# Two transformer blocks on one core: no wait for the attention's stores, another order of vector work in the gated linear attention, and mixer tiles three steps ahead of their product

## The chip, the cores and the metric

One core of one Trainium2 chip runs the whole program in one launch. The metric is the device time of an execution in microseconds (us). The engines are TensorE (PE in the profile; PEld is its weight load), VectorE (DVE), ScalarE (ACT), GpSimd (POOL) and SyncE (SP), whose queue issues the DMA transfers. Each engine runs its own list of instructions in the order in which they were written, and waits on semaphores for the others.

## The reference, cut to what matters

The program computes two blocks, one after the other, on 1024 tokens of width 1024, in float32. The first is a gated delta-rule mixer (8 heads of 128) and a squared-ReLU MLP (width 4096). The second has a softmax attention (8 query heads of 64, 2 key heads, 1280 keys: 256 of a context and 1024 of the sequence), a bidirectional gated linear attention ("GLA", called hgrn2 in the reference, 4 heads of 128), an output projection of both, and a SwiGLU MLP (2 x 2816).

```
def gated_deltanet(...):                       # first block
    ...  8 heads, chunks of 128 tokens in the kernel, output o
    return (o * rsqrt(mean(o*o)+eps) * norm_w * silu(z)) @ w_out

def hgrn2_prep(q, i, f, lb_d):                 # second block, GLA
    fg = lb_d + (1.0 - lb_d) * sigmoid(f)
    qh = silu(q) * 128 ** -0.5
    return qh, 1.0 - fg, i, log(fg)            # queries, keys, values, log decay
S_t = diag(f_t) S_{t-1} + k_t v_t^T;  o_t = S_t^T q_t     # forward and backward
o = rmsnorm(o_f + flip(o_b), gain) * silu(g)
x = x + mx[2] * (concat([att_x, hg_x]) @ w_out)
```

Both parts are linear in the values i, so the factor 128 ** -0.5 may stand on the queries or on the values.

## The kernel before, in words

Activations are kept feature-major: a tile is 128 features by 1024 tokens. A large product runs in three passes (high and low halves of weights and of activations), in "units" of one 128-wide output tile: a unit has 8 k-steps, each in two "pieces". For every unit SP loads 512 KB of weights (`sp_weights`, L461), ACT copies the high half (`act_weights`, L478) and DVE subtracts to get the low half (`dve_weights`, L486). PE may start a unit when DVE's part is done. There are three buffers of each.

The order of the work is written out by hand. While a recurrent chain runs, with many short hand-overs between PE, ACT, DVE and POOL, large products of the next head fill PE. They come from a generator of steps (`DeltaSide` for the first block's mixer, `GlaSide` for the second's). Every engine calls the same generator at the same points (`side.fill(n)` runs n steps, `side.until(x)` runs them until x is ready). A step gives PE one piece; the other engines get their own share of the unit at its start and end. A `yield` without work before it is a step in which PE gets nothing. When the chain is over, `side.finish()` runs what is left.

The last steps of both generators are `mix_steps` (L151): the first two output tiles (i = 0, 1) of the output projection, over k-tiles 0 to 6 of the mixer's output. These k-tiles lie in device memory and are loaded again (`sp_mix`). `mix_tile(k)` makes ACT copy the high half of k-tile k (L1310) and DVE subtract the low half (L1316); `mix_piece` is PE's share (by `gemm_piece`, L497), four or two matmuls of 512 columns. `mix_tile(0)` waits for the end of the last unit before, since it overwrites that unit's activations. k-tile 7 comes from the last head at the end (L1323, L1328, and L1354 on PE). In the first block the steps begin in head 7, at the fourth turn of its two half chains (`delta_halves`, L813). There L1125 and L1127 are small DVE sums and L1139 is the first DVE copy of the triangular inversion; L930 on PE and L1180 on DVE end the head. In the second block they begin in GLA head 3, at the sixth of its seven levels.

The softmax attention (`*_attend`, L2092 to L2229) makes 160 steps of scores, exponentials and products with the values; SP stores its output tiles (L2099) to device memory. At its end each engine calls `after_attend` (L2103), which waits for all events of this stage and for all of these stores. Only then does an engine enter the GLA, whose tiles lie in the same on-chip memory. In the GLA the projections of head 0 come first (L2806 is PE's piece, L2849 is ACT's evacuation into the head's tile, by `gla_into`, L2334; L2816 and L2866 transpose the values).

A GLA head then runs so. DVE waits for the queries of the head, for the store of the previous head's output (`glast`) and for POOL, scales the queries (L2456), makes the decay factors and keys of both directions (L2459, L2461, twice) and adds the keys (L2463, event "kk"). PE multiplies keys and queries (L2279, event "dg"). DVE puts the diagonal (L2445) and makes the two decayed queries (L2469, event "q0"). Then come 7 levels: PE L2292, DVE and POOL multiply keys (L2423), queries (L2430) and factors (L2433), DVE puts the level's part (L2445), ACT makes the interleaved keys (L2404, L2407). Then follow transposes of the keys (L2304), the states (L2310 on PE, L2486 and L2492 on DVE), the output (L2319 to L2321) and its norm and gate (L2501 to L2514, event "of"). SP stores it (L2254). `gla_fill` is the number of fill steps at each point; in head 3 it is halved.

Of the kernel before, what the change touches and what calls it, by code (L numbers as in the profile page):

```python
# [10 lines left out]
ALU = mybir.AluOpType  # L11
# [7 lines left out]
KT = 8  # L19
# [131 lines left out]
def mix_steps(on):  # L151

    on.mix_tile(0)
    for k in range(KT - 1):
        if k + 1 < KT - 1:
            on.mix_tile(k + 1)
        for part in range(2):
            for i in range(2):
                on.mix_piece(i, k, part)
                yield None  # L160
# [165 lines left out]
class Kernel:  # L326
# [1765 lines left out]
    def sp_attend(self, e):  # L2092
        P, A, V, G = self.at
        for i in range(16):
# [3 lines left out]
            for p in range(2):  # L2098
                e.dma_start(self.scratch[0][64 * p:64 * p + 64, 2 * g:2 * g + 2, qc],  # L2099
                            ao[:, :, p, :]).then_inc(*self.attst[i % 4].up(i, p))  # L2100
        self.after_attend(e)

# [6 lines left out]
    def pe_attend(self, e):  # L2109
# [21 lines left out]
        for t in range(162):  # L2131
# [14 lines left out]
            if t >= 2:  # L2146
# [3 lines left out]
                if b == 0 and i >= 2:  # L2150
                    e.wait_ge(*V.at("of", i - 2))
                e.matmul(O[i % 2], self.vx[:, b, 64 * g:64 * g + 128], self.prob[(t - 2) % 4], start=b == 0,  # L2152
                         stop=b == 9).then_inc(*P.up("pv", t - 2))
        self.after_attend(e)

    def act_attend(self, e):
        P, A, V, G = self.at
        MX, MT, S, O = self.attend_banks()
        for t in range(160):
# [3 lines left out]
            e.activation(self.prob[t % 4], S[t % 3], ACT.Exp, scale=0.125).then_inc(*A.up("ex", t))  # L2163
        self.after_attend(e)

    def dve_attend(self, e):
# [28 lines left out]
        for i in range(17):  # L2195
# [18 lines left out]
            if i < 15:  # L2214
                maxima(i + 1, 2)
                maxima(i + 1, 3)
                shift(i + 1)
        self.after_attend(e)

    def pool_attend(self, e):  # L2220
# [4 lines left out]
        for i in range(16):  # L2225
            qc, g, r, base = self.attend_rows(i)
            e.wait_ge(*(P.at("s", 10 * (i - 2) + 9) if i >= 2 else G.at("zero", g)))
            e.tensor_copy(self.qx[g][r], self.qs[g][r, :, qc].bitcast(F32)).then_inc(*G.up("qx", i))
        self.after_attend(e)  # L2229

# [16 lines left out]
    def sp_gla(self, e):  # L2247
        V = self.gs[2]
        e.dma_start(self.masks, self.a["masks"]).then_inc(*self.maskl.up("gla"))
        j0 = UNIT["win", 10]  # L2250
# [15 lines left out]
    def pe_gla(self, e):  # L2266
# [4 lines left out]
        for h in range(4):  # L2271
# [4 lines left out]
            side.fill(self.gla_fill(h, 8))  # L2276
            e.wait_ge(*V.at("kk", h))
            for n in range(8):
                ins = e.matmul(blk(D0, n), blk(B["sq"], n), blk(B["hq"], n), start=True, stop=True)  # L2279
# [54 lines left out]
    def gla_into(self, e, u, c):  # L2334
        P, A, V, G = self.gs
        i = u[1] - 6
        part, h = i // 4, i % 4
        if part == 1:
            if h >= 2:
                e.wait_ge(*P.at("o", h - 2))  # L2340
            return self.iv[h % 2].rearrange("p a b -> p (a b)")[:, c], ACT.Copy
# [93 lines left out]
    def dve_gla(self, e):  # L2435
# [11 lines left out]
        for h in range(4):  # L2447
            side.stage = 4 * h
            side.until((h, "hq"))
            f = {n: B[f"f{n}{h % 2}"] for n in "fb"}  # L2450
            k, q = {"f": B["kf"], "b": B["kb"]}, {"f": B["qf"], "b": B["qb"]}
            e.wait_ge(*A.at("ev", ("win", 6 + h), 1))
            if h:
                e.wait_ge(*self.glast.at(h - 1))
                e.wait_ge(*G.at("up", h - 1, 6))
            e.tensor_scalar(B["hq"], B["hq"], 128.0 ** -0.5, None, ALU.mult)  # L2456
            for d, n in enumerate("fb"):
                j = 4 * d + h
                e.tensor_scalar(f[n], f[n], self.olb[:, j:j + 1], self.lb[:, j:j + 1], ALU.mult, ALU.add).then_inc(*V.up())  # L2459
                e.wait_ge(*V.last())  # L2460
                e.tensor_scalar(k[n], f[n], -1.0, 1.0, ALU.mult, ALU.add).then_inc(*V.up())  # L2461
            e.wait_ge(*V.last())
            e.tensor_tensor(B["sq"], k["f"][:, TC:TA], k["b"][:, TC:TA], ALU.add).then_inc(*V.up("kk", h))  # L2463
            side.fill(self.gla_fill(h, 8))
            e.wait_ge(*P.at("dg", h))
            side.fill(self.gla_fill(h, 3))
            put(self.con("ident"), D0, "put", h, "d")
            for n in "fb":
                ins = e.tensor_tensor(q[n], B["hq"], f[n][:, TC:TA], ALU.mult)  # L2469
# [356 lines left out]
class ActSide:  # L2826
# [27 lines left out]
    def turned(self, u):  # L2854
# [3 lines left out]
        for j in range(3):  # L2858
            n = min(4, 10 - 4 * j)
            if u == ("win", 5):  # L2860
# [5 lines left out]
            e.activation(out[:, 4 * j:4 * j + n, :], s.ps[:, 512 * j:512 * j + 128 * n].rearrange("p (b m) -> p b m", b=n),  # L2866
                         ACT.Copy).then_inc(*self.sig[1].up("tv", u, j))

# [175 lines left out]
```

## Time and profile before

| | us |
|---|---|
| median of 3 runs | 3335.62 (3332.84 to 3340.41) |
| the profiled execution's own time | 3333.01 |
| its span | 3331.2 |
| PE busy | 3100.7 (93%) |
| DVE busy | 1553.6 (47%) |
| ACT busy | 1002.6 (30%) |
| POOL busy | 433.9 (13%) |
| matmuls of the large products, L497 | 1474.4 in 5928 |
| matmuls of the projections, L2806 | 363.9 in 1584 |

The span is the time from the first to the last instruction; 1.8 us of the execution lie around it. Busy time of PE counts a matmul from start to a modelled end, so it says where PE had work, and not that it ran at its peak. The mean granted clock of PE was 0.973 of full speed.

### The profile page before, as it was taken

What the parts mean: (1) busy time and instruction counts of PE and PEld (TensorE: products, weight loads), DVE (VectorE), ACT (ScalarE), POOL (GpSimd) and SP (SyncE); (2) the same over time, 40 slices, a digit from 0 to 9 for tenths busy, and PEclk for the clock granted to TensorE, in tenths of its full rate; (3) what the DMA queues carried; (4) which work ended last, traced back from release to release, by engine and by line L of the source; (5) the groups of instructions that cost most, each with busy time, mean ns of one, the idle gap of its engine ahead of it and who ended that gap; (6) DMA issues with size and microseconds to landing.
All of it is one profiled execution on the core that took longest, in us unless ns stands there. A gap on an engine that the chain in (4) does not pass through costs nothing. (4 is left out here: it accounts for less than half of the span.)

```text
span 3331.2 us, 36380 instructions
## 1 busy us (share of the span) xinstructions
PE 3100.7 (93%) x15051; PEld 2518.8 (76%) x15051; DVE 1553.6 (47%) x1912; ACT 1002.6 (30%) x1440; POOL 433.9 (13%) x343
## 2 busy tenths in 40 slices
PE   7899999979999999999688998989879999999998
PEld 5788888867788888887565666877767788888886
DVE  7566656652664543333456761654463322222223
ACT  5555555542211111112423332222222211111111
POOL 4222223221000000001100000332131000000001
PEclk9999999999999999999888999999999999999999
DMA  3111111112233331112110001010012111111111
GB/s 124 33 45 45 45 45 45 45 64 102 89 108 120 114 97 49 50 46 87 42 51 5 9 10 41 20 38 32 26 58 100 42 47 50 46 51 45 51 43 59
DMA packets 77237, 184.78 MB, mean 55 GB/s; under 512 B 7056, under 2 KB 29072, under 8 KB 77072
## 3 DMA queue, kind: packets, MB, share of 16 engines
q1 hardware_dynamic: 77072, 182.44, 17.5%
q8 instruction: 120, 1.97, 0.3%
q14 instruction: 45, 0.37, 0.0%
HBM read 163.87 MB, written 15.79 MB: 54 GB/s over the span
## 5 line engine op out<-in xcount | busy, mean ns | idle before, releaser
L497 PE MATMUL ps<-b 128*128 128x512 f32 x5928 | 1474.4, 399 | 46.4 <-DVE b L1316 15.0
L497 PEld LDWEIGHTS ps<-b 128*128 128x128 f32 x5928 | 1091.3, 190 | 259.4 <-issue 26.8
L1512 PE MATMUL ps<-b 128*128 128x512 f32 x2592 | 608.5, 395 | 0.5 <-DVE b L1643 0.5
L1512 PEld LDWEIGHTS ps<-b 128*128 128x128 f32 x2592 | 485.1, 187 | 119.0 <-DVE b L1643 1.0
L486 DVE TENSOR_TENSOR b<-b 128x1024 fp32r<-128x1024 f32 (+1 forms) x206 | 254.7, 1237 | 326.9 <-ACT b L478 319.9
L2806 PE MATMUL ps<-b 128*128 128x512 f32 (+1 forms) x1584 | 363.9, 386 | 37.1 <-DVE b L1866 14.4
L478 ACT ACTIVATE b<-b 128x1024 fp32r<-128x1024 f32 (+1 forms) x206 | 215.1, 1045 | 562.7 <-PE ps L1512 463.8
L2806 PEld LDWEIGHTS ps<-b 128*128 128x128 f32 x1584 | 283.6, 197 | 94.8 <-issue 42.7
L1381 POOL TENSOR_TENSOR b<-b 128x1024 f32<-128x1024 f32 x24 | 57.5, 2397 | 1642.7 <-ACT b L1387 1642.3
L1558 ACT ACTIVATE b<-ps 128x1024 f32<-128x1024 f32 x54 | 55.4, 1025 | 389.2 <-PE ps L497 389.2
L2152 PE MATMUL ps<-b 128*128 128x512 f32 x320 | 163.0, 592 | 0.0
L1659 DVE TENSOR_TENSOR b<-b,ps 128x1024 f32<-128x1024 f32 x64 | 78.1, 1220 | 168.5 <-PE ps L1512 168.5
L2163 ACT ACTIVATE b<-ps 128x512 f32<-128x512 f32 x160 | 95.3, 597 | 149.2 <-PE ps L2145 149.2
L1564 ACT ACTIVATE b<-b 128x1024 fp32r<-128x1024 f32 x54 | 57.3, 1061 | 261.5 <-DVE b L1638 216.5
L1661 DVE SCALAR_TENSOR_TENSOR b<-ps,b 128x1024 f32<-128x1024 f32 x48 | 61.6, 1284 | 149.6 <-PE ps L1512 149.6
L1640 DVE TENSOR_TENSOR b<-b 128x1024 f32<-128x1024 f32 x32 | 39.2, 1225 | 183.1 <-ACT b L1558 183.1
L2176 DVE TENSOR_REDUCE b<-ps 128x1 f32<-128x1280 f32 x64 | 95.3, 1489 | 46.6 <-PE ps L2120 46.2
L1223 POOL TENSOR_TENSOR b<-b 128x256 f32<-128x256 f32 x96 | 82.6, 864 | 198.7 <-DVE b L1111 115.7
L2752 DVE SCALAR_TENSOR_TENSOR b<-b 128x1024 f32<-128x1024 f32 x72 | 105.3, 1463 | 0.8
L1638 DVE TENSOR_TENSOR b<-b,ps 128x1024 f32<-128x1024 f32 x22 | 26.9, 1221 | 166.2 <-PE ps L497 162.5
L2144 PE MATMUL ps<-b 128*128 128x512 f32 x160 | 98.2, 614 | 0.0
L1643 DVE TENSOR_TENSOR b<-b 128x1024 fp32r<-128x1024 f32 x54 | 66.2, 1225 | 60.8 <-ACT b L1564 60.8
(291 smaller groups left out, 3297.1 us busy)
## 6 DMA issues: line engine op xcount, KB each, us to landing
b<-in_down SPq DMA_DIRECT2D x52, 512.0 KB, 3.6
b<-in_mod SPq DMA_DIRECT2D x96, 256.0 KB, 2.7
b<-in_gu SPq DMA_DIRECT2D x44, 512.0 KB, 3.6
b<-scratch SPq DMA_DIRECT2D x38, 512.0 KB, 4.4
b<-in_dn_in SPq DMA_DIRECT2D x32, 512.0 KB, 4.9
b<-in_up SPq DMA_DIRECT2D x32, 512.0 KB, 3.7
b<-in_win SPq DMA_DIRECT2D x26, 512.0 KB, 4.0
scratch<-b SPq DMA_DIRECT2D x18, 512.0 KB, 3.0
```

The source lines that it names most:

```text
L478: e.activation(self.whi[j % SPL][:, 0:cols], self.raw[j % RAW][:, 0:cols], ACT.Copy).then_inc(*self.wh.up(j))
L486: e.tensor_tensor(self.wlo[j % SPL][:, 0:cols], self.raw[j % RAW][:, 0:cols], self.whi[j % SPL][:, 0:cols].bitcast(F32), ALU.subtract).the ...
L497: ins = e.matmul(ps[:, c], w, h[:, k, c], start=first and k == 0 and i == 0, stop=last and k == KT - 1 and i == 2)
L1223: e.tensor_tensor(out, own, m.broadcast_to([128, 4, 64 >> lv, 1 << lv]), ALU.mult).then_inc(*G.up("m", h, lv, f))
L1512: ins = e.matmul(ps[:, c], w, u[:, at[k], c], start=k == 0 and p == 0, stop=k == n - 1 and p == 2)
L1659: e.tensor_tensor(x, x, ps, ALU.add).then_inc(*V.up("down", f, i))
L2144: e.matmul(S[t % 3], blk(self.ks[g], b), self.qs[g][:, :, qc], start=True, stop=False)
L2152: e.matmul(O[i % 2], self.vx[:, b, 64 * g:64 * g + 128], self.prob[(t - 2) % 4], start=b == 0, stop=b == 9).then_inc(*P.up("pv", t - 2))
L2163: e.activation(self.prob[t % 4], S[t % 3], ACT.Exp, scale=0.125).then_inc(*A.up("ex", t))
L2176: e.tensor_reduce(mx[:, j:j + 1], MX, AX.X, ALU.max).then_inc(*V.up("mx", i, j))
L2752: e.scalar_tensor_tensor(out=dst, in0=k.d_pad[c % 2][:, t:t + T], scalar=cw[:, t:t + 1], in1=dst, op0=ALU.mult, op1=ALU.add).then_inc(*V.u ...
L2806: ins = e.matmul(self.bank[p], (hi, hi, lo)[i], x, start=k == 0 and i == 0, stop=last)
```

## The change

There are four edits.

1. `after_attend` is no longer called by PE, DVE and POOL at the end of the attention. ACT calls it before its first evacuation of head 0's values (the first write into a tile of the GLA), SP at the start of `sp_gla`. In its old place SP calls `sp_weights` with a bound that the projections before have reached already.
2. In `dve_gla` the factors, keys and their sum are made as soon as both gates of the head are projected (`side.until((h, "b"))`), with a wait for the evacuated gates, ahead of the waits for the queries, for the previous head's store and for POOL. These three waits now stand before the decayed queries (L2469). PE waits for the evacuated queries itself before L2279.
3. The queries are not scaled (L2456 goes). ACT scales the values by the same factor as it evacuates their transpose (L2866).
4. `mix_steps` starts with three steps in which PE gets nothing: `mix_tile(0)` in the first, `mix_tile(1)` in the second, none in the third. The later tiles keep their place relative to the pieces.

```
 def mix_steps(on):
     on.mix_tile(0)
+    yield None
+    on.mix_tile(1)
+    yield None
+    yield None
     for k in range(KT - 1):
-        if k + 1 < KT - 1:
+        if 0 < k < KT - 2:
             on.mix_tile(k + 1)
...
 def sp_attend(self, e):
-        self.after_attend(e)
+        self.sp_weights(e, UNIT["win", 10] + 4)
 # pe_attend, act_attend, dve_attend, pool_attend:
-        self.after_attend(e)
 def sp_gla(self, e):
         V = self.gs[2]
+        self.after_attend(e)
         e.dma_start(self.masks, self.a["masks"])...
 # pe_gla
             e.wait_ge(*V.at("kk", h))
+            e.wait_ge(*A.at("ev", ("win", 6 + h), 1))
 # gla_into
         if part == 1:
+            if h == 0 and c.start == TC:
+                self.after_attend(e)
 # dve_gla
         for h in range(4):
-            side.stage = 4 * h
-            side.until((h, "hq"))
             f = {n: B[f"f{n}{h % 2}"] for n in "fb"}
             k, q = {"f": B["kf"], "b": B["kb"]}, {"f": B["qf"], "b": B["qb"]}
-            e.wait_ge(*A.at("ev", ("win", 6 + h), 1))
-            if h:
-                e.wait_ge(*self.glast.at(h - 1))
-                e.wait_ge(*G.at("up", h - 1, 6))
-            e.tensor_scalar(B["hq"], B["hq"], 128.0 ** -0.5, None, ALU.mult)
+            side.stage = 4 * h
+            side.until((h, "b"))
             for d, n in enumerate("fb"):
                 j = 4 * d + h
+                e.wait_ge(*A.at("ev", ("win", 14 + j), 2))
                 e.tensor_scalar(f[n], f[n], self.olb[...], self.lb[...], ALU.mult, ALU.add)
                 e.wait_ge(*V.last())
                 e.tensor_scalar(k[n], f[n], -1.0, 1.0, ALU.mult, ALU.add)
             e.wait_ge(*V.last())
             e.tensor_tensor(B["sq"], k["f"][:, TC:TA], k["b"][:, TC:TA], ALU.add).then_inc(*V.up("kk", h))
+            side.until((h, "hq"))
             side.fill(self.gla_fill(h, 8))
             e.wait_ge(*P.at("dg", h))
             side.fill(self.gla_fill(h, 3))
             put(self.con("ident"), D0, "put", h, "d")
+            e.wait_ge(*A.at("ev", ("win", 6 + h), 1))
+            if h:
+                e.wait_ge(*self.glast.at(h - 1))
+                e.wait_ge(*G.at("up", h - 1, 6))
             for n in "fb":
                 ins = e.tensor_tensor(q[n], B["hq"], f[n][:, TC:TA], ALU.mult)
 # ActSide.turned
-                         ACT.Copy)
+                         ACT.Copy, scale=128.0 ** -0.5)
```

## Rows read from the trace of the kernel before

**Rows 1.** page, section 1: busy time of each engine, share of the span, instructions.
```profile
PE 3100.7 (93%) x15051; PEld 2518.8 (76%) x15051; DVE 1553.6 (47%) x1912; ACT 1002.6 (30%) x1440; POOL 433.9 (13%) x343
```

**Rows 2.** waits of TensorE's matmuls, 2010 to 2560: us in total, times, longest.
```profile
PE ps L2279 <- DVE b L2463: 17.8, 4, 7.3
...
PE ps L2806 <- DMA scratch<-b: 7.1, 1, 7.1
PE ps L497 <- DVE b L1316: 5.4, 1, 5.4
```

**Rows 3.** the same view, 676 to 752 (delta head 7 and what follows).
```profile
PE ps L497 <- DVE b L1316: 9.6, 1, 9.6
...
PE ps L1354 <- DVE b L1328: 1.4, 1, 1.4
PE ps L930 <- DVE b L1173: 0.9, 1, 0.9
```

**Rows 4.** timeline at the attention's end: start us, us, instruction, [idle before <-releaser].
```profile
2005.76 13.56 SPq L2099 DMA_DIRECT2D scratch<-b  x4
...
2011.20 2.74 PE L2152 MATMUL ps<-b 128*128 128x512 f32 x6
...
2021.02 16.93 PE L2806 MATMUL ps<-b 128*128 128x512 f32 x72 [7.08 <-DMA scratch<-b]
...
2024.79 1.23 DVE L486 TENSOR_TENSOR b<-b 128x1024 fp32r<-128x1024 f32 x1 [6.72 <-DMA b<-in_masks]
```

**Rows 5.** windows: stretch, length, busy us (count) by engine, TensorE clock, DMA.
```profile
693.00:747.80 54.80, 47.69 (x306) 39.15 (x304) 27.97 (x63) 22.01 (x54) 12.28 (x12) 1.00 0.07 20
...
2021.00:2027.00 6.00, 5.98 (x17) 4.93 (x18) 1.23 (x1) 1.06 (x1) 0.00 (x0) 0.50 0.50 165
```

**Rows 6.** timeline, GLA head 0: the keys' product.
```profile
2088.05 2.05 PE L2279 MATMUL ps<-b 128*128 128x128 f32 x16 [1.47 <-DVE b L2463]
```

**Rows 7.** timeline, change from GLA head 0 to head 1.
```profile
2184.84 1.28 DVE L2514 SCALAR_TENSOR_TENSOR b<-b 128x1024 f32<-128x1024 f32 x1
...
2189.20 0.69 DVE L2456 TENSOR_SCALAR b<-b 128x1024 f32<-128x1024 f32 x1 [3.08 <-DMA scratch<-b]
...
2194.64 3.47 PE L2279 MATMUL ps<-b 128*128 128x128 f32 x16 [5.64 <-DVE b L2463]
...
2196.81 1.23 DVE L486 TENSOR_TENSOR b<-b 128x1024 fp32r<-128x1024 f32 x1 [2.22 <-ACT b L478]
...
2198.15 1.32 DVE L2445 COPY_PREDICATED b<-b,ps 128x1024 f32<-128x1024 uint32 x1
...
2201.76 2.92 PE L2292 MATMUL ps<-b 128*128 128x128 f32 x16 [1.37 <-DVE b L2469]
```

**Rows 8.** timeline, change to head 2 (first row) and to head 3.
```profile
2304.92 2.05 PE L2279 MATMUL ps<-b 128*128 128x128 f32 x16 [3.36 <-DVE b L2463]
...
2401.73 1.28 DVE L2514 SCALAR_TENSOR_TENSOR b<-b 128x1024 f32<-128x1024 f32 x1
...
2411.52 3.78 PE L2279 MATMUL ps<-b 128*128 128x128 f32 x16 [7.32 <-DVE b L2463]
```

**Rows 9.** timeline, GLA head 3 where the output projection begins.
```profile
2451.87 2.35 DVE L1316 TENSOR_TENSOR b<-b 128x1024 fp32r<-128x1024 f32 x2
...
2458.01 0.69 DVE L2430 TENSOR_TENSOR b<-b 128x512 f32<-128x512 f32 x1 [3.05 <-PE ps L2292]
...
2490.72 4.82 PE L497 MATMUL ps<-b 128*128 128x512 f32 x20
```

**Rows 10.** timeline, delta head 7 where the output projection begins.
```profile
684.98 3.20 DVE L1316 TENSOR_TENSOR b<-b 128x1024 fp32r<-128x1024 f32 x2
...
687.19 2.04 PE L497 MATMUL ps<-b 128*128 128x512 f32 x4 [9.59 <-DVE b L1316]
...
694.20 0.23 DVE L1139 COPY b<-b 128x128 f32<-128x128 f32 x1 [2.56 <-PE ps L876]
```

**Rows 11.** line 1316: instructions, duration ns min/median/max, first and last start.
```profile
L1316 DVE TENSOR_TENSOR b<-b x14: 1172/1221/2062, 685.0 to 2488.8; 128x1024 fp32r<-128x1024 f32 x14
```

More of the change, by code:

```diff
@@ L153, in mix_steps @@
     on.mix_tile(0)
+    yield None
+    on.mix_tile(1)
+    yield None
+    yield None
     for k in range(KT - 1):
-        if k + 1 < KT - 1:
+        if 0 < k < KT - 2:
             on.mix_tile(k + 1)
@@ L2100, in sp_attend @@
                             ao[:, :, p, :]).then_inc(*self.attst[i % 4].up(i, p))
-        self.after_attend(e)
+        self.sp_weights(e, UNIT["win", 10] + 4)
     def after_attend(self, e):
@@ L2153, in pe_attend @@
                          stop=b == 9).then_inc(*P.up("pv", t - 2))
-        self.after_attend(e)
     def act_attend(self, e):
@@ L2163, in act_attend @@
             e.activation(self.prob[t % 4], S[t % 3], ACT.Exp, scale=0.125).then_inc(*A.up("ex", t))
-        self.after_attend(e)
     def dve_attend(self, e):
@@ L2217, in dve_attend @@
                 shift(i + 1)
-        self.after_attend(e)
     def pool_attend(self, e):
@@ L2228, in pool_attend @@
             e.tensor_copy(self.qx[g][r], self.qs[g][r, :, qc].bitcast(F32)).then_inc(*G.up("qx", i))
-        self.after_attend(e)
     GLA_ORDER = {"f": list(range(9)), "b": [1, 0, 9, 8, 7, 6, 5, 4, 3]}
@@ L2248, in sp_gla @@
         V = self.gs[2]
+        self.after_attend(e)
         e.dma_start(self.masks, self.a["masks"]).then_inc(*self.maskl.up("gla"))
@@ L2277, in pe_gla @@
             e.wait_ge(*V.at("kk", h))
+            e.wait_ge(*A.at("ev", ("win", 6 + h), 1))
             for n in range(8):
@@ L2338, in gla_into @@
         if part == 1:
+            if h == 0 and c.start == TC:
+                self.after_attend(e)
             if h >= 2:
@@ L2447, in dve_gla @@
         for h in range(4):
-            side.stage = 4 * h
-            side.until((h, "hq"))
             f = {n: B[f"f{n}{h % 2}"] for n in "fb"}
             k, q = {"f": B["kf"], "b": B["kb"]}, {"f": B["qf"], "b": B["qb"]}
[L2452 to L2456, printed above, removed]
+            side.stage = 4 * h
+            side.until((h, "b"))
             for d, n in enumerate("fb"):
                 j = 4 * d + h
+                e.wait_ge(*A.at("ev", ("win", 14 + j), 2))
                 e.tensor_scalar(f[n], f[n], self.olb[:, j:j + 1], self.lb[:, j:j + 1], ALU.mult, ALU.add).then_inc(*V.up())
@@ L2463, in dve_gla @@
             e.tensor_tensor(B["sq"], k["f"][:, TC:TA], k["b"][:, TC:TA], ALU.add).then_inc(*V.up("kk", h))
+            side.until((h, "hq"))
             side.fill(self.gla_fill(h, 8))
@@ L2467, in dve_gla @@
             put(self.con("ident"), D0, "put", h, "d")
+            e.wait_ge(*A.at("ev", ("win", 6 + h), 1))
+            if h:
+                e.wait_ge(*self.glast.at(h - 1))
+                e.wait_ge(*G.at("up", h - 1, 6))
             for n in "fb":
@@ L2866, in turned @@
             e.activation(out[:, 4 * j:4 * j + n, :], s.ps[:, 512 * j:512 * j + 128 * n].rearrange("p (b m) -> p b m", b=n),
-                         ACT.Copy).then_inc(*self.sig[1].up("tv", u, j))
+                         ACT.Copy, scale=128.0 ** -0.5).then_inc(*self.sig[1].up("tv", u, j))
 class DveSide:
```

## The prediction

> **What bounds the kernel now.** I read the page first: PE is busy in 93% of the span [rows 1]. So a change off PE counts only where PE waits, or where PE runs at half clock behind a wait. Next I read PE's own waits in the two stretches that the diff touches. In the GLA the longest are those for the keys' sum (17.8 us, 4 times), for the attention's stores (7.1, once) and for the first tile of the output projection (5.4, once) [rows 2]. In delta head 7 it is that first tile again (9.6, once), and behind it two small ones of 1.4 and 0.9 [rows 3]. Each is then looked up in the timeline, for what stood ahead of the late instruction on its own engine. All in all the diff touches 17.8 + 7.1 + 5.4 + 9.6 = 39.9 us of stalls. The sum is made against the profiled execution: 3331.2 us of span and 1.8 around it, 3333.0. The median of three runs, 3335.6, lies 2.6 above that.
>
> **Edit 1, the attention's end.** PE's last product ends at 2013.9 and the first projection begins at 2021.0, when the last stores have landed [rows 4]. The weights of the first two units are made already, and PSUM is free. After the change PE goes on at once: 7.1 us less. The projection then began at the 1.2 GHz level: 6.0 us with a granted clock of 0.50 [rows 5], work that takes 3.0 us at 2.4 GHz. With no pause there is no reason for that fall: 3.0 less. Sum: 10.1.
> What is late next? ACT takes over the wait, ahead of its first evacuation. Behind it are queued that evacuation and later weight copies; PE waits for the evacuation. The projection takes 16.93 - 3.0 = 13.9 us, so it ends at 2027.9, some 7 us after the stores. The wait is hidden; if the stores landed 10 us later it would cost 3. SP issues the load of the masks after the same stores as before, and DVE makes the third unit's low half behind it, 2024.8 to 2026.0 [rows 4]. PE needs it after two units, at 2013.9 + 2 x 13.9 = 2041.7, so this is hidden as well. The moved SP call issues nothing. Bounds: 7.1 (the clock falls anyway) to 10.1; I take 10.1.
>
> **Edits 2 and 3, the heads' beginnings.** Head 0: PE waits 1.47 us for the keys' sum [rows 6]. Its gates are evacuated one projection earlier, so DVE's work lies beside the queries' projection: 1.5 less.
> Head 1: DVE ends the head before at 2186.1, waits 3.08 us for its store, scales queries for 0.69, and makes factors and keys until 2194.6 [rows 7]. The first two go from this place, 3.8, and 4.75 are left of the 8.5. PE had sat idle for 5.64, so this is all gain at the keys' product. Is it kept until the levels? The diagonal on DVE waits for that product and, through a fill step, for one weight split (L486), which starts when ACT is through its key copies and a weight copy, also released by the keys' sum. It ended 3.4 us after the sum [rows 7], and will again. The diagonal and the queries follow. So the first level, at 2201.76, comes 3.8 earlier. The store has landed by 2189.2, before the decayed queries need their tile (about 2195.7): the moved wait is hidden, by 6 us.
> Head 2: the same step, but PE waited only 3.36 [rows 8]; no weight split stands in between here, and I take 3.4.
> Head 3: DVE ended at 2403.0, so the sum comes at about 2407.8 in place of 2411.5. The keys' product ran 3.78 us at half clock [rows 8] and held the diagonal until 2415.3; now the weight split holds it, until 2407.8 + 3.4 = 2411.2. That gives 4.1.
> The factor on the values rides on a copy that is made in any case. The trace shows no such copy with a factor; its bound is from 0 to the 0.69 of the scaling that goes [rows 7], three per head, beside other waits; I take 0. PE's added wait for the evacuated queries comes 8 or 4 fill steps after the projection: 0, at most about 1 in head 0. Sum: 1.5 + 3.8 + 3.4 + 4.1 = 12.8. Bounds: 6 (half of it is met by the next link of the chain, since the wait for the decayed queries, 1.37 in head 1, stays) to 15.
>
> **Edit 4 in GLA head 3.** PE sat 5.4 us before the first piece; level 7 had to wait behind it [rows 2]. Now level 7 is issued first. DVE becomes the limit: after level 6 it splits weights and tile 0, then multiplies the keys and waits for PE. Gone from its chain are half of the two tile splits (2.35 / 2) and the 3.05 of idle before the level's queries [rows 9]: 4.2. But three steps of PE's work, which lay here, move to the end. By the order of the pieces the steps now left over are of 4, 2 and 2 matmuls, at 4.82 / 20 = 0.24 each [rows 9]: 1.9. The 20 matmuls at the end covered the last tile's preparation fully (there is no wait for it there), so nothing absorbs them. Net 2.3. Bounds: -2 (the chain meets other waits and the three steps are pure cost) to 4.2.
>
> **Edit 4 in delta head 7.** PE's first piece started at 687.19 after 9.59 us. It needed DVE's first tile split, which ended about 687, and DVE's arrival there was not set by PE [rows 10]. So this piece starts no earlier. What changes is the work around it: the second half chain's transposes, and both halves' next ones, pass ahead of it and fill the pause. The chain's next link on DVE (L1139) stood at 694.20. Now it follows the first piece (2.04 at half clock) and one short transpose group (about 0.4): 687.2 + 2.0 + 0.5 = 689.7. DVE's own list reaches it in time: split until 687.0, two small sums of 0.9, the second split 1.2, 689.1. So the chain is 4.5 ahead. From 693 to 747.8 PE is busy for 47.7 of 54.8 us [rows 5] with the same steps at the same points, so the lead is passed on. At the end come three steps more, 8 matmuls, 1.9 us; the 0.9 before L930 [rows 3] absorbs half. Net 4.5 - 1.0 = 3.5. The 1.4 before the last tile stays, being DVE's. Bounds: -1 (no lead, the work only displaced, 1.0 exposed) to 6.5 (clock stays up).
> A rule on the split's length: line 1316 takes 1.22 at the median, and 2.06 at its longest, here in head 7 [rows 11]. The Trainium skill, GPSIMD Engine Reference, section 1 "Specifications", has GpSimd share its SBUF interfaces with VectorE, with contention for DVE instructions with two SBUF inputs. By that rule the first split stays long, since the change moves nothing of GpSimd's work away; if it dropped to 1.22 the sum would be 0.8 larger. I leave it long.
>
> **Sum.** 10.1 + 12.8 + 2.3 + 3.5 = 28.7. The profiled execution would take 3333.0 - 28.7 = 3304.3, a median like the one shown 3306.9. I say 3305.5, between them.
>
> **Rivals.**
> A. *The pieces are missed.* Removing three steps of fill under two latency-bound chains gives nothing or costs: -1 and -2 in place of 3.5 and 2.3, so 28.7 - 8.8 = 19.9, at 3314. For it: PE has only about 7 us of idle in 693 to 747.8, so the displaced steps find little room. Against it: both waits are ended by work queued on DVE, that is there in the rows.
> B. *The heads' waits move on.* The keys' sum comes early but the decayed queries are then late, behind the weight split, the store or ACT: half of the 12.8 is lost, 3312. For it: the wait before the first level was there each time. Against: all that stands ahead of it is released by the same sum.
> C. *The handover is hidden anyway*, or the edit does not do what it says: ACT, now holding the wait, stops PE at its first evacuation, or PE waits for the third unit. Then the 10.1 goes, 3315.6. Against it are the 7 and 15 us of slack.
> D. *The clock gives more.* After the pauses in heads 1 and 3 and in head 7 PE ran at the lower level; if it no longer falls there, 3 in the delta head and 3 to 5 in the GLA come on top: 3298.
> E. *Slower.* In head 7 the long stall made PE fall to half clock and it came back by 693. In the new order it falls in the shorter pause, has no large piece in turn 4, and stays at the 1.2 GHz level through the whole chain. Four matmuls of a piece took 2.04 at that level [rows 10] against 4 x 0.24 + 0.2 = 1.2 at the other, a factor of 1.7; on 47.7 us of work that is 33, at 3305.5 + 33 = 3338, slower. It decides from 41 us at half clock on (28.7 / 0.7). Against it: the same work in 693 to 747.8 was granted 1.00 throughout [rows 5].
>
> **How the numbers follow.** Forecast 0.60, its own range 3299 to 3311; A 0.11; B 0.10; C 0.05; D 0.10; E 0.02; nothing to be measured 0.02. Two measurements of this kernel are told apart from about 0.2%, 6.7 us. The range goes from D's far side to C and A together with a part of B: 3293 to 3321. What is left out is mostly E, pairs of A, B and C, and terms that I have not seen. Faster by over 0.2%: 0.94; within it: 0.03; slower: 0.03.
>
> **What would show it.** PE goes from the attention's last product to the first projection within 1 us, and all of that projection runs at clock 1.00; its transposes wait no longer than now. PE's waits for the keys' sum fall from 17.8 to about 5 (heads 1 and 3: about 2 and 3.6; heads 0 and 2: none). The first levels of heads 1 to 3 come 3 to 4 us closer to the end of the head before. In GLA head 3 PE's level 7 comes before any L497; the pause of 5.4 is replaced by two of 1.5 and 3.5. In delta head 7 the pause before the first piece is 4 to 5, and the pieces after the last head's output are 16 matmuls in place of 8. It would be wrong if a wait of over 3 us appeared before a first level or before L2816, or if the stretch between the fourth turn of head 7 and the last tile were not shorter.

## The result, and the profile after

The changed kernel took 3310.3 us (median of 4 runs, 3306.1 to 3311.3) against 3335.8 for the kernel before on the same chip (4 runs, 3332.8 to 3340.4): a ratio of 0.992, 95% interval 0.990 to 0.994. The forecast was 3305.5, with its own range of 3299 to 3311 and 3293 to 3321 in all, so the result lies at the upper edge of the first. Taken again beside other kernels, the same code took 3308.6 against 3337.0, ratio 0.9913 (0.9899 to 0.9927). All executions behind the medians here are fast ones, and the single slow one, 8833.1 us with the kernel that has the wait for the stores put back, is left out. The profiled execution took 3311.3, with a span of 3309.3: 21.9 less than before. The changed lines stand a few lines lower: L497 is now L501, L1316 is L1320, L2279 is L2281, L2292 is L2294, L2469 is L2474, L2806 is L2811, L2152 is L2156, L486 is L490, L1139 is L1143, L1354 is L1358, L2304 is L2306, L2430 is L2434, L2445 is L2449, L2492 is L2497, L2514 is L2519; L2463 stays.

The page's first section, kernel after, beside [rows 1]:

```profile
PE 3106.2 (94%) x15051; PEld 2523.6 (76%) x15051; DVE 1549.6 (47%) x1908; ACT 1003.0 (30%) x1440; POOL 435.5 (13%) x343
```

As many products as before and four DVE operations less, the four scalings of the queries. PE's busy time is 5.5 us higher: those are the same products, a few more of them at half clock (121.9 us of PE's busy time lie in stretches of half clock, in place of 109.7). So not all of PE's idle time that went came off the span.

I cut both executions at instructions that both have. D runs in delta head 7 from PE's last value transposes to the first product of the last k-tile (L1354 before). H runs from the start of the attention's last products to the keys' product of GLA head 0. K1, K2, K3 run from the broadcast of the norms (L79) to the first level's product of GLA heads 1, 2, 3. G runs in GLA head 3 from the sixth level's product to the first product of the last k-tile.

| stretch | before | after | gain | forecast |
|---|---|---|---|---|
| D | 72.30 | 66.25 | 6.05 | 3.5 |
| H | 76.85 | 65.23 | 11.62 | 10.1 + 1.5 |
| K1, K2, K3 | 19.30, 18.13, 20.21 | 15.42, 14.53, 16.00 | 3.9, 3.6, 4.2 | 3.8, 3.4, 4.1 |
| G | 50.06 | 51.68 | -1.6 | +2.3 |
| all the rest | 3074.4 | 3080.2 | -5.8 | 0 |

The touched stretches give 27.7, against 28.7 forecast. The rest is the same instructions in the same order, and is longer by 2.3 ahead of D, by 2.2 between D and H and by 1.4 elsewhere. It differs by such amounts between executions of one code: the stretch between D and H took 1265.6 in this one and 1264.1 in the second profile of the same kernel, 1261.8 and 1265.4 in the two profiles of another, and from 1258.0 to 1265.6 over all the profiles here. There is only one profile of the kernel before, so that the change adds nothing there is likely and not shown.

Waits of PE's matmuls, kernel after, 1980 to 2560 (us in total, times, longest), beside [rows 2]:

```profile
PE ps L2294 <- DVE b L2474: 8.9, 4, 2.7
...
PE ps L2281 <- DVE b L2463: 4.0, 2, 3.6
...
PE ps L2306 <- DVE b L2434: 3.2, 1, 3.2
...
PE ps L2294 <- DVE b L2434: 2.5, 2, 1.5
...
PE ps L501 <- DVE b L1320: 0.4, 1, 0.4
PE ps L2306 <- DVE b L2449: 0.4, 1, 0.4
```

The 17.8 for the keys' sum are 4.0, the 7.1 for the stores are no longer there, and the 5.4 before the first piece have become 1.5 before level 7 (L2294, of the 2.5), and 3.2 and 0.4 behind it, before the transposes of the keys (L2306). The forecast had two pauses of 1.5 and 3.5 there. The row on top has grown a little: PE waits in each head for the decayed queries (L2474), as it did before (7.3 in the same view, 4 times). In head 1 it was 1.37 [rows 7] and is 2.6.

### The profile page after: what moved, and what is told of

It reads as the page before. It is cut to its first block and busy times, and to the rows that moved or that the text cites. A ratio compares the mean times of both kernels' runs of the same rounds, so it can differ in the third digit from the quotient of the medians.

```text
span 3309.3 us, 36368 instructions
## 1 busy us (share of the span) xinstructions
PE 3106.2 (94%) x15051; PEld 2523.6 (76%) x15051; DVE 1549.6 (47%) x1908; ACT 1003.0 (30%) x1440; POOL 435.5 (13%) x343
## 3 DMA queue, kind: packets, MB, share of 16 engines
q1 hardware_dynamic: 77072, 182.44, 17.4%
## 5 line engine op out<-in xcount | busy, mean ns | idle before, releaser
L501 PE MATMUL ps<-b 128*128 128x512 f32 x5928 | 1478.5, 400 | 37.6 <-DVE b L490 13.7
L501 PEld LDWEIGHTS ps<-b 128*128 128x128 f32 x5928 | 1095.4, 191 | 252.1 <-issue 17.2
L490 DVE TENSOR_TENSOR b<-b 128x1024 fp32r<-128x1024 f32 (+1 forms) x206 | 255.2, 1240 | 313.3 <-ACT b L482 306.1
L2811 PE MATMUL ps<-b 128*128 128x512 f32 (+1 forms) x1584 | 364.8, 387 | 30.1 <-DVE b L1870 14.4
L2811 PEld LDWEIGHTS ps<-b 128*128 128x128 f32 x1584 | 283.9, 197 | 87.8 <-issue 35.3
L2156 PE MATMUL ps<-b 128*128 128x512 f32 x320 | 163.4, 593 | 0.0
L2178 DVE TENSOR_REDUCE b<-ps 128x1 f32<-128x1280 f32 x64 | 95.3, 1489 | 47.6 <-PE ps L2124 47.2
```

Of the source, the lines that this page charges most:

```text
L490: e.tensor_tensor(self.wlo[j % SPL][:, 0:cols], self.raw[j % RAW][:, 0:cols], self.whi[j % SPL][:, 0:cols].bitcast(F32), ALU.subtract).the ...
L501: ins = e.matmul(ps[:, c], w, h[:, k, c], start=first and k == 0 and i == 0, stop=last and k == KT - 1 and i == 2)
L2178: e.tensor_reduce(mx[:, j:j + 1], MX, AX.X, ALU.max).then_inc(*V.up("mx", i, j))
L2811: ins = e.matmul(self.bank[p], (hi, hi, lo)[i], x, start=k == 0 and i == 0, stop=last)
```

## The experiments

Each kernel is the changed one with the edit shown, timed in five rounds beside the kernel before. They ran in three sets, each on a chip of its own: the first four kernels, the next four (the products in both places, the changed kernel again, the wait put back, the old order of keys), and the rest. Where a text gives a time it is the kernel's median.

**The lead taken back, in both places and in the GLA alone.** For the second, the four gated heads' projections got a generator of their own with the old order.

```diff
 def mix_steps(on):
     on.mix_tile(0)
-    yield None
-    on.mix_tile(1)
-    yield None
-    yield None
     for k in range(KT - 1):
-        if 0 < k < KT - 2:
+        if k + 1 < KT - 1:
             on.mix_tile(k + 1)
```

> The changed kernel without edit 4 in either block: the first pieces of both output projections come right behind the last unit, as before. Two stretches are read. D goes from the transposes of the values in delta head 7 (72.3 us before, 66.2 changed) to the product with k-tile 7; G from the sixth level's product in GLA head 3 (50.1 before, 51.7 changed) to the same. My theory: edit 4 is worth 6.0 in D and costs 1.6 in G, and nothing outside of them. Then D is 72.3, G 50.1, and the time about 3314.7 against 3310.3 for the changed kernel. Rival: the differences in D and G come from where the earlier edits shift the loads of tiles and weights. Then G stays near 51.7 with the old order, or D below 70.

> The changed kernel with edit 4 in the delta mixer alone; the GLA has the old order of mixer tiles. My theory: D 66.2, G 50.1, so 1.6 faster than the changed kernel, about 3308.7. Rival: G only looks longer because the stretch behind it got shorter (the same work, read at another point); then the time is the changed kernel's 3310.3 or more, and the stretch from the sixth level to the end of the program is as long as in the changed kernel or longer.

Without any lead: 3313.2 (3311.4 to 3313.6), D 72.27, G 49.96. With the lead in the delta rule alone: 3307.1, D 66.15, G 50.03. So the lead is worth 6.1 in the delta rule, and costs 1.7 in the GLA: with it G is 51.68 and 51.79 in the two profiles of the changed kernel. In the delta rule it can be more: D is 65.07 in the second of these profiles, where the clock came back sooner. From the sixth level to the end of the program the kernel with the old order in the GLA took 885.9, the changed one 888.3, so the rival falls too. H and the three K were as in the changed kernel in both (65.2; 15.3 to 15.8, 14.5, 15.8), so edit 4 and the others do not lean on each other.

**A lead of one step in the GLA.** Tile 1 follows one step behind tile 0, and the two further empty steps go.

```diff
+def mix_steps_gla(on):
+    on.mix_tile(0)
+    yield None
+    on.mix_tile(1)
+    for k in range(KT - 1):
+        if 0 < k < KT - 2:
+            ...                  # as in mix_steps
```

> The changed kernel with one empty step in place of three in the GLA: the seventh level's product still passes ahead of the first piece, but the first two pieces lie in PE's pause behind it. Theory 1 (the three steps go to the end, where nothing absorbs them, and the pause of 3.2 lets the clock fall for the pieces behind it): the pause is filled, the ten matmuls after the transposes of the keys take 2.5 in place of 4.1, G is 51.7 - 1.9 (8 matmuls fewer at the end) - 2.2 (clock) = 47.6, and the time about 3306. Rival (the clock is not part of it, DVE's list is): the pause only moves, G is 49.8 at best, 3308.5.

3305.0 (3303.2 to 3309.6), G 50.90: it missed the 47.6 of the first theory by far. It lies 1.1 above the best that the rival allowed, but the rival held the clock to be no part of it, and the rows say otherwise. The timeline shows why. DVE, then PE, of this kernel (L1334 is the tile's split, L515 the pieces):

```profile
2425.61 2.09 DVE L1334 TENSOR_TENSOR b<-b 128x1024 fp32r<-128x1024 f32 x1
...
2430.53 1.22 DVE L1334 TENSOR_TENSOR b<-b 128x1024 fp32r<-128x1024 f32 x1
```

```profile
2427.85 3.43 PE L515 MATMUL ps<-b 128*128 128x512 f32 x8 [2.76 <-DVE b L1334]
...
2440.59 4.12 PE L515 MATMUL ps<-b 128*128 128x512 f32 x10
```

PE waited 2.76 us, for a split that took 2.09 beside GpSimd's part of the level (its L2448 and L2451 were running), and then did eight products in 3.43, where eight take 2.1 at full clock. Later ten took 4.12, where they take 2.53 at full clock. Both the pause and the clock stand in this result.

**The pause filled with products that are thrown away.** In GLA head 3, 12 products of 128x512 follow level 7 and fill the pause ahead of the keys' transposes; they go to PSUM that the first piece overwrites.

```diff
     on.mix_tile(1)
+    on.warm(6)
     yield None
+    on.warm(6)
     yield None
```

> The changed kernel with 12 matmuls of 512 columns in the second and third empty step of the GLA, whose results are thrown away; PE has this work in the pause behind the seventh level's product and nothing else differs. Clock theory: no fall, the ten matmuls after the transposes of the keys take 2.5 in place of 4.1, the eight of those transposes 1.0 in place of 2.0, G is about 49.5. Rival (these matmuls are slow by the loads of the mixer tiles into on-chip memory at that time, or their modelled ends): they stay at 4.1 and G at 51.7 or above.

3305.9 (G 48.47). The window over the whole stretch G in this kernel (length, busy us and count of PE, PEld, DVE, ACT, POOL, clock, DMA), and below it the window of the changed kernel in which its first ten products fall:

```profile
2415.00:2464.00 49.00, 42.04 (x257) 35.60 (x258) 30.18 (x45) 17.40 (x22) 9.28 (x8) 1.00 0.17 46
```

```profile
2430.00:2436.00 6.00, 5.49 (x17) 4.42 (x18) 3.46 (x4) 2.14 (x3) 1.25 (x2) 0.50 0.43 134
```

The pieces' first ten products, here and in the changed kernel:

```profile
2427.16 2.54 PE L519 MATMUL ps<-b 128*128 128x512 f32 x10
```

```profile
2420.97 2.02 PE L2294 MATMUL ps<-b 128*128 128x128 f32 x16 [0.81 <-DVE b L2437]
...
2424.95 2.05 PE L2294 MATMUL ps<-b 128*128 128x128 f32 x16 [1.48 <-DVE b L2434]
2430.15 1.97 PE L2306 MATMUL ps<-b 128*128 128x128 f32 x8 [3.15 <-DVE b L2434]
2432.48 0.48 PE L2306 MATMUL ps<-b 128*128 128x128 f32 x1 [0.36 <-DVE b L2449]
2432.69 4.12 PE L501 MATMUL ps<-b 128*128 128x512 f32 x10
...
2442.36 1.65 PE L2306 MATMUL ps<-b 128*128 128x128 f32 x9 [2.14 <-DVE b L2497]
2443.65 3.33 PE L501 MATMUL ps<-b 128*128 128x512 f32 x8
```

With the clock at 1.00 throughout, G is 1.6 less than in the old order. How much of that is the early tile by itself stays open, since the old order has a stretch of half clock of its own (below). In the changed kernel the clock fell twice, in the pause before 2430 and around 2443. Ten products took 4.12 in place of 2.54 and eight 3.33 in place of 2.08, 2.8 us in all, and most of 51.68 - 48.47 = 3.2.

**The same in both places, and the changed kernel again.** In delta head 7, 24 products are thrown away as well, in four lots around the tiles' preparation.

```diff
     on.mix_tile(0)
+    on.warm(2)
     yield None
     on.mix_tile(1)
+    on.warm(2)
     yield None
+    on.warm(4)
     yield None
+    on.warm(16)
```

> The changed kernel with matmuls whose results are thrown away in the pauses that edit 4 leaves: 12 in the GLA as in the run before (2 and 3 of the empty steps), and 24 in delta head 7 (2, 2 and 4 in its empty steps and 16 ahead of the first piece, where PE sat idle for 4.7 us). Clock theory: the first pieces in delta head 7 take 1.2 each in place of 2.0, D is 66.2 - 2 = 64.2, G 48.5, and the time 3310.3 - 2.0 - 3.2 = 3305. Rival: in the delta head the chain is bound by DVE's list, so a faster clock there only lengthens PE's waits and D stays within 65.5 to 66.3.

> The changed kernel once more, beside the others on the same chip. D 66.2, G 51.7, 65.2 from the attention's last product to the first keys' product, as in its first profile; 3310.3. If a stretch differs by more than 1 between the two profiles of one program, that is what a difference of one stretch between two kernels must exceed.

3303.9 (3302.2 to 3306.9) beside 3308.6 (3305.9 to 3313.0) of the changed kernel. D fell to 63.63. In delta head 7 of the changed kernel, and then of this one:

```profile
689.49 2.04 PE L501 MATMUL ps<-b 128*128 128x512 f32 x4 [4.66 <-DVE b L1320]
...
692.47 2.05 PE L501 MATMUL ps<-b 128*128 128x512 f32 x4
```

```profile
690.38 1.16 PE L523 MATMUL ps<-b 128*128 128x512 f32 x4 [1.01 <-DVE b L1342]
...
691.97 1.18 PE L523 MATMUL ps<-b 128*128 128x512 f32 x4
```

Two pieces take 1.75 less, and D is 2.6 less than in the first profile of the changed kernel and 1.4 less than in the second. There the first piece took 2.04 again, but the clock was back before the second:

```profile
692.13 1.29 PE L501 MATMUL ps<-b 128*128 128x512 f32 x4
```

So D differs by 1.2 between two executions of one kernel, and how long the half clock lasted tells them apart. The granted clock in 688 to 696 is 0.54 and 0.73 in the two profiles of the changed kernel and 1.00 here. The time came out near the expected 3305, but the two stretches did not: D gained more, and G was 51.64 in place of 48.5, with the same instructions in GLA head 3 as in the kernel whose G was 48.47. The ten products again, in this kernel, and their window:

```profile
2423.53 4.11 PE L523 MATMUL ps<-b 128*128 128x512 f32 x10
```

```profile
2423.00:2428.00 5.00, 4.68 (x16) 3.84 (x17) 1.37 (x2) 1.36 (x3) 0.00 (x0) 0.66 0.35 105
```

**That kernel once more.** The kernel with 12 thrown-away products in the GLA alone, letter for letter.

> The kernel with 12 products thrown away in the pauses of gated head 3, letter for letter the one that ran before (G 48.5 us with the clock at 1.00 throughout); the kernel with thrown-away products in both places had the same instructions in that stretch, with the clock at half for a part and G 51.6. My theory: whether the clock falls there differs from one execution to the next and the products don't hold it: G comes out anywhere from 48.5 to 51.7, time 3305 to 3308. Rival: it is the kernel that decides, and G is 48.5 again.

3308.1 (3303.8 to 3308.9), G 51.47, with the ten products at 4.11. The rival falls: the code does not decide it. One code gave 48.47 and 51.47. The two profiles are of two chips, so the chip is not excluded by them. But on both chips the executions of this code differ among themselves, with mean clocks of 0.974 to 0.977 and times of 3302.8 to 3309.8 on the first and 3303.8 to 3308.9 on the second.

**The old order in the GLA, with the products in the delta rule.** Once with 14 thrown-away products behind level 6 of GLA head 3, once without.

```diff
+def mix_steps_gla(on):
     on.mix_tile(0)
+    on.warm(14)                  # not in the second kernel
     for k in range(KT - 1):
         if k + 1 < KT - 1:
             on.mix_tile(k + 1)
```

> The changed kernel with the delta rule's products thrown away in the pauses as in the fastest kernel so far (24 products of 512 columns), and with the old order of tiles in the four gated heads' projections, where 14 products are thrown away behind level 6 of head 3 and ahead of the first piece; their results are overwritten. D is the delta rule's last head up to its last k-tile's products (66.3 us in the changed kernel, 63.6 with the thrown-away products), G the stretch in gated head 3 from its sixth level's product to the products of k-tile 7 (50.1 before, 51.7 changed, 50.0 with the old order alone, 48.5 with the early tile and a clock that stayed at 1.00). My theory: the early tile loses because the pause that it makes is followed by the half clock; the old order has a 2.5 us wait and no such fall, so the thrown-away products change nothing: D 63.6, G 50.0, about 3302 us. Rival: a half clock is in the old order's G too and the products take it away: G 48.5, 3300.5.

> The same kernel without the 14 products in gated head 3: the old order of tiles there, the three-step lead and the thrown-away products in the delta rule alone. My theory: D 63.6, G 50.0, about 3302 us, and within 1 us of the kernel with the 14 products. Rival: G is 51.7 here too, so that the early tile was not what lengthened it, and the time is 3304.

3304.8 and 3305.8, with D 63.62 and 63.61, G 49.93 and 50.05. The old order has its half clock too: in 2425 to 2430 the clock was 0.66 and 0.65. There it meets the four products of the first piece (1.81 and 2.04 in place of 1.2) and a level of short ones, and the 14 products do not keep it away. My "no such fall" was wrong; that G stays at 50.0 held. The rival's half clock was there, but the products did not take it away.

**The wait for the stores put back** where it was, on all five engines.

```diff
-        self.sp_weights(e, UNIT["win", 10] + 4)
+        self.after_attend(e)
 # and behind the attention of PE, ACT, DVE and POOL
+        self.after_attend(e)
 # and out of sp_gla and gla_into again
```

> The changed kernel without edit 1: all engines wait for the attention's stores again. Read is H, from the last product of the attention to the first keys' product (76.85 before, 65.23 changed). Theory: 10.1 of the difference are the wait of 7.1 and the half clock behind it (3.0), the rest is the earlier keys in head 0. H is 75.3, the time 3320.4. Rival 1: the clock falls for another reason there, so H is 72.3. Rival 2: the wait is hidden by something else than stated, H below 70.

H 74.20, where 75.3 was expected; 3316.8 (five executions, 3313.6 to 3320.2; ratio 0.9937, 0.9923 to 0.9951). The first projection in this kernel and in the changed one:

```profile
2014.60 15.91 PE L2812 MATMUL ps<-b 128*128 128x512 f32 x72 [7.08 <-DMA scratch<-b]
```

```profile
2009.59 2.74 PE L2156 MATMUL ps<-b 128*128 128x512 f32 x6
2011.76 14.57 PE L2811 MATMUL ps<-b 128*128 128x512 f32 x72
```

The wait is back to the hundredth, 7.08. The projection takes 14.57 at the granted clock of 1.00 and 16.93 [rows 4] or 15.91 behind the pause, so the half clock cost 2.4 before and 1.3 here, where the forecast had 3.0. In the changed kernel the projection also overlaps the end of the attention's last product by 0.6 (2.17 from start to start, where the group takes 2.74). The sum is 7.1 + 2.4 + 0.6 + 1.5 for the keys' sum = 11.6, as measured.

**The old order of queries, factors and keys,** the scale staying on the values.

```diff
-            side.until((h, "b"))
+            side.until((h, "hq"))
+            e.wait_ge(*A.at("ev", ("win", 6 + h), 1))
+            if h:
+                e.wait_ge(*self.glast.at(h - 1))
+                e.wait_ge(*G.at("up", h - 1, 6))
 ...                             # the same waits taken out further down
```

> The changed kernel without edit 2, with edit 3: DVE waits for the queries, the previous head's store and POOL ahead of factors and keys, and no scaling of the queries is left. Read are H and, for heads 1 to 3, K: from the broadcast of the norm in the head before to the first level's product (19.3, 18.1, 20.2 before; 15.4, 14.5, 16.0 changed). Theory: the scaling was in the chain for its 0.69 and the store's wait for the rest: H 66.0, K 18.6, 17.4, 19.5, the time 3320.5. Rival: the factor on the values costs ACT time or the scaling was beside the chain, then K is as before, 19.3, 18.1, 20.2, and the time 3322.5.

3320.6 (3315.2 to 3324.7), H 66.24, K 19.40, 19.11, 19.02, in place of 15.4, 14.5 and 15.7 to 16.0 in the changed kernel's two profiles: 3.0 to 4.6 a head. The 19.11 is 1 more than the kernel before had in head 2; here the keys' product ran at half clock there (3.03 against 2.05). Taken together the K fit neither the theory (18.6, 17.4, 19.5) nor the rival (19.3, 18.1, 20.2), so this kernel does not settle what the missing scaling is worth. On DVE it is gone: from the head before (L2514, here L2518) to the keys' sum head 1 takes 7.9 in place of 8.5. But the keys' product took 3.78 there at half clock, and the diagonal waited 0.42 for it. PE's waits for the keys' sum are back, in the same view as above:

```profile
PE ps L2281 <- DVE b L2467: 16.0, 4, 7.8
PE ps L2294 <- DVE b L2473: 6.1, 4, 2.7
```

**The scale on the queries again,** with the new order and no factor on the values. This kernel leaves the scale off the diagonal's terms, which are multiplied before it.

```diff
+            e.tensor_scalar(B["hq"], B["hq"], 128.0 ** -0.5, None, ALU.mult).then_inc(*V.up())
+            e.wait_ge(*V.last())
             for n in "fb":
 ...
-                         ACT.Copy, scale=128.0 ** -0.5)
+                         ACT.Copy)
```

> The changed kernel with the scale 128^-0.5 back on the queries: one VectorE operation on 128x1024 fp32 ahead of the decayed queries in each gated head, with no scale on the value copies. K is the time from the broadcast of the norms to the first level's product in heads 1, 2, 3 (15.4, 14.5, 16.0 us in the changed kernel). My theory: the operation stands on the chain between the copy of the diagonal and the two products for the decayed queries, and TensorE's level 0 waits for these, so K grows by the time of that operation, 0.7 us a head: 16.1, 15.2, 16.7, and head 0 by as much, 2.7 us in all, 3311 us. Rival: it lies in the time in which VectorE waits for the diagonal product anyway, because the placed work ahead of it moves; K unchanged and 3308.5 us.

3312.5 (3305.1 to 3314.5), K 16.92, 15.26, 16.93; head 0's step from the keys' product to its first level grew from 5.60 to 6.33. DVE in head 1:

```profile
2179.73 1.30 DVE L2449 COPY_PREDICATED b<-b,ps 128x1024 f32<-128x1024 uint32 x1
2180.92 0.68 DVE L2473 TENSOR_SCALAR b<-b 128x1024 f32<-128x1024 f32 x1
2181.63 2.36 DVE L2476 TENSOR_TENSOR b<-b 128x1024 f32<-128x1024 f32 x2
```

The operation of 0.68 pushes the decayed queries back, and the first level by 0.7 in heads 0 and 2, by 0.9 in head 3 and by 1.5 in head 1. There 0.8 of it came ahead of the keys' product: the broadcast of the norms fell into a stretch of half clock and took 1.96 in place of 1.17. So the scaling is on the path where this kernel has it, and the factor on the copies costs nothing. The copies of ScalarE before and after (line, times: ns min/median/max):

```profile
L2866 ACT ACTIVATE b<-ps x12: 385/577/597, 2039.9 to 2340.6; 128x512 f32<-128x512 f32 x8, 128x256 f32<-128x256 f32 x4
```

```profile
L2871 ACT ACTIVATE b<-ps x12: 385/579/597, 2028.3 to 2319.6; 128x512 f32<-128x512 f32 x8, 128x256 f32<-128x256 f32 x4
```

## Why the prediction was right, and where not

**Edit 1 (10.1).** Right. PE goes from the attention's last product to the projection without a gap, in 2012 to 2027 the clock is 1.00, and the transposes behind it wait 0.6. The wait on ACT is hidden and the third unit is not late. Of the 3.0 put down to the clock, 2.4 is that: the 6.0 us at half clock were not twice what the same products need at full clock. The 0.6 of overlap, which the forecast did not have, makes up for it, so that the 10.1 came out to the tenth is partly luck.

**Edits 2 and 3 (12.8).** Right in each head: 1.5, 3.9, 3.6 and 4.2 against 1.5, 3.8, 3.4 and 4.1 (4.0, 3.6 and 4.5 by the second profile). Head 1 shows the chain that the forecast named. DVE, then PE, of the kernel after:

```profile
2171.43 1.28 DVE L2519 SCALAR_TENSOR_TENSOR b<-b 128x1024 f32<-128x1024 f32 x1
2172.63 0.94 DVE L2459 TENSOR_SCALAR b<-b 128x1280 f32<-128x1280 f32 x1
...
2176.18 1.23 DVE L2463 TENSOR_TENSOR b<-b 128x1024 f32<-128x1024 f32 x1
2179.66 1.23 DVE L490 TENSOR_TENSOR b<-b 128x1024 fp32r<-128x1024 f32 x1 [2.25 <-ACT b L482]
2180.80 1.30 DVE L2449 COPY_PREDICATED b<-b,ps 128x1024 f32<-128x1024 uint32 x1
2181.99 2.35 DVE L2474 TENSOR_TENSOR b<-b 128x1024 f32<-128x1024 f32 x2
```

```profile
2177.47 2.05 PE L2281 MATMUL ps<-b 128*128 128x128 f32 x16 [0.34 <-DVE b L2463]
...
2184.39 2.92 PE L2294 MATMUL ps<-b 128*128 128x128 f32 x16 [2.58 <-DVE b L2474]
```

Between the head before (L2519) and the factors DVE stands idle no more. The weight split (L490) ends 3.5 us after the sum, against 3.4 in [rows 7], as it waits for ACT; behind it come the diagonal and the queries. They are DVE's own work from the sum on, except for those 2.25 us, and that is why nothing was lost at the next link (rival B), though PE's wait there grew.

**Edit 4 in GLA head 3 (2.3): the term that failed, with the wrong sign.** The forecast reckoned a lead of 4.2 on DVE's chain and 1.9 of displaced products, all at full clock. The lead came: level 7 starts 4.0 behind the sixth level's product in place of 9.8, and the keys' transposes 9.2 behind it in place of 13.9, 4.7 earlier. The 1.9 came, with 0.45 of wait before the last of these. What failed is that the step priced only work and waits. Rival D reckoned that the clock could only be better without the long pause; it cost more, as the pause is now followed by the transposes and ten large products in a row in place of four. In the one execution whose clock stayed up, G was 1.6 below the old order with its own half clock (50.1 to 48.5); the forecast's 2.3 was not reached there either. In all profiles with the new order of tiles in the GLA and its three-step lead, G was 51.7, 51.8, 51.6, 49.4, 51.6, 51.5, 51.5 and 48.5; in the five with the old one it was 49.9 to 50.1. The high ones have the ten products at 3.8 to 4.1, the 48.5 at 2.5, and the 49.4 at 3.3.
What remains open is what makes the clock fall in one execution and not in another. The Trainium skill, TensorE: Matmul & The Clock Gate, Part 1, says that the monitor behind the gate runs freely and is not reset by the kernel, so that the same code meets it at different points. The two executions of one code here agree with that: 48.5 and 51.5.

**Edit 4 in delta head 7 (3.5): right mechanism, too small by 2.5 (by 3.7 in the second profile).** The lead is 4.5 as forecast: from the value transposes to L1139/L1143 it was 18.71 us and is 14.23. The displaced products are there, 16 in place of 8 at the end, and the wait for L930 is gone. What I left out are PE's other small waits inside the chain. They stand in the views of waits, 684 to 748 before, 686 to 742 after:

```profile
PE ps L901 <- ACT b L1028: 2.1, 6, 0.5
PE ps L876 <- DVE b L1143: 1.7, 4, 0.8
...
PE ps L930 <- DVE b L1173: 0.9, 1, 0.9
```

```profile
PE ps L905 <- ACT b L1032: 1.2, 6, 0.2
PE ps L920 <- ACT b L1040: 0.2, 1, 0.2
```

From 2.1 + 1.7 + 0.9 and 0.5 of smaller ones, 5.2, to 1.4. With these, 4.5 + 3.8 - 1.9 = 6.4, near the 6.05 measured. That they went because tile 2's split no longer stands on DVE between two links (696.3 before) is likely, and I did not test it. Rival E, the half clock through the whole chain, did not come: one or two pieces ran at it, and against the kernel without it D is 1.4 and 2.6 longer. The first split stayed at 2.06 beside GpSimd, as the forecast assumed, and the second took 1.22. In the GLA with a lead of one step one was again 2.09 beside GpSimd and the next 1.22 without. The rule on the shared interfaces in the Trainium skill, GPSIMD Engine Reference, section 1 "Specifications", agrees with these. But it is not always DVE that pays. GpSimd, then DVE, of the changed kernel, in delta head 7 and in GLA head 3:

```profile
681.18 2.35 POOL L1234 TENSOR_TENSOR b<-b 128x512 f32<-128x512 f32 x2
...
685.17 3.10 POOL L1234 TENSOR_TENSOR b<-b 128x512 f32<-128x512 f32 x2
...
2423.08 1.27 POOL L2434 TENSOR_TENSOR b<-b 128x512 f32<-128x512 f32 x1 [0.34 <-PE ps L2294]
...
2427.08 3.94 POOL L2434 TENSOR_TENSOR b<-b 128x512 f32<-128x512 f32 x1 [0.65 <-PE ps L2294]
```

```profile
686.15 1.21 DVE L490 TENSOR_TENSOR b<-b 128x1024 fp32r<-128x1024 f32 x1
687.28 2.06 DVE L1320 TENSOR_TENSOR b<-b 128x1024 fp32r<-128x1024 f32 x1
...
2427.54 1.22 DVE L1320 TENSOR_TENSOR b<-b 128x1024 fp32r<-128x1024 f32 x1
```

The weight split of the same shape took 1.21 beside GpSimd's pair at 685.17, which took 3.10 where the pair before had taken 2.35. In the GLA tile 0's split took 1.22, and GpSimd's operation beside it 3.94 in place of 1.27.

So the forecast of the whole, 28.7, was close to the 27.7 of the touched stretches partly by luck: two errors were opposite, -3.9 in the GLA and +2.5 in the delta rule. Most of the distance, from 3304.3 to 3311.3 for the profiled execution, is the 5.8 of stretches that the change does not touch, and which vary from execution to execution.

**A version with a shorter delta head 7.** The thrown-away products in delta head 7 gave D 63.6 three times out of three, against 66.3 and 65.1 in the changed kernel. The three kernels that have them took 3303.9, 3304.8 and 3305.8; their ratios to the kernel before, 0.9899, 0.9911 and 0.9911, have intervals that overlap that of the changed kernel, 0.9913. So the gain over it is shown in the stretch, and not in the time of the whole.

## What to carry to other kernels

A wait that goes is worth what the next link leaves of it: read on the engine that ended it how much of the following chain hangs on the same event. Here that gave each head to 0.2 us, and to 0.4 in the second profile. When small fill is taken out of a pause, look at what comes behind the pause: large products in a row there pay for a fallen clock (ten took 4.1 us in place of 2.5). Whether a chain that waits for another engine anyway pays less was not measured here. And sum the many small waits of a latency-bound chain as well as the large one at its head.

## What the runs showed of the hardware that I had not expected

In GLA head 3 of the changed kernel the granted clock was 0.50 from the pause of 3.15 us on, though PE's waits from 2415 up to that pause were 1.5 us at most; in 2430 to 2436 PE was busy for 5.49 of 6 us. With 12 products put into the pause it still fell in two executions of three, behind waits of 0.4 and 1.2 us. In the third, with the same waits, it stayed at 1.00 throughout. Ten products of 128x512 take 2.54 or 4.11 by that, and the whole stretch 48.5 or 51.5. A factor on ScalarE's copy of 128x512 costs nothing that shows: 579 ns against 577. And of a VectorE and a GpSimd operation side by side, both with two inputs in the on-chip memory, either can be the one that gets longer: 2.06 in place of 1.21 us on VectorE, or 3.94 in place of 1.27 on GpSimd.
